# Two transformer blocks on one core: in the second routed layer, the weight pieces of two experts alternate in groups of eight

## The reference

```python
def moe_swiglu(x, w_router, w_gate, w_up, w_down):
    logits = (x @ w_router).astype(jnp.float32)
    top_val, top_idx = lax.top_k(logits, TOP_K)          # TOP_K = 2
    top_w = jax.nn.softmax(top_val, axis=-1)
    gate = jnp.einsum('bsk,bske->bse', top_w,
                      jax.nn.one_hot(top_idx, N_EXPERTS_2, dtype=jnp.float32)).astype(x.dtype)
    y = jnp.zeros_like(x)
    for e in range(N_EXPERTS_2):                         # 8 experts, inner width 3584
        h = jax.nn.silu(x @ w_gate[e]) * (x @ w_up[e])
        y = y + gate[..., e:e + 1] * (h @ w_down[e])
    return y
```

## Time and profile before

| | |
|---|---|
| three runs | 2212.12, 2214.03 (median), 2217.06 us |
| the profiled execution's own time | 2219.89 us |
| its span | 2218.1 us |
| TensorE busy | 2043.3 us (92%) |
| VectorE, ScalarE busy | 1248.8 us (56%), 991.1 us (45%) |
| HBM traffic over the span | 270 GB/s mean |
| this layer | from about 1236 us to about 2200 us |
| the three pairs | from about 1384 us to about 2094 us |

### The profile page before, as it was taken

How to read it: one execution, slowest core, us unless ns; L and a number is a source line. 1 busy time by engine, 2 the same in 40 slices (tenths; PEclk the granted TensorE clock), 3 DMA queues, 4 the chain that set the end, 5 groups by cost and what they waited for, 6 DMA issues and landing times. The chain is left out here.

```text
span 2218.1 us, 29794 instructions
## 1 busy us (share of the span) xinstructions
PE 2043.3 (92%) x11784; PEld 1520.7 (69%) x11784; DVE 1248.8 (56%) x1928; ACT 991.1 (45%) x1399; POOL 163.0 (7%) x151
## 2 busy tenths in 40 slices
PE   8998899999898889999989899999989998999896
PEld 8996885443687778997858687656645655665685
DVE  4557652221446676676276788544544544554787
ACT  3555442111244554442274567434443444443683
POOL 2103100000000003431001000000000000000000
PEclk9998998999998999999999999999999999999998
DMA  8650539999663244557502599999999999999994
GB/s 264 186 171 1 170 117 396 417 416 417 239 215 96 77 135 144 200 176 178 149 20 96 212 330 383 382 398 383 402 405 380 386 399 414 384 388 402 383 370 166
DMA packets 228364, 601.35 MB, mean 271 GB/s; under 512 B 16091, under 2 KB 121967, under 8 KB 205568
## 3 DMA queue, kind: packets, MB, share of 16 engines
q1 hardware_dynamic: 220112, 571.56, 69.0%
q0 software_dynamic: 8112, 27.91, 3.9%
HBM read 594.37 MB, written 5.05 MB: 270 GB/s over the span
## 5 line engine op out<-in xcount | busy, mean ns | idle before, releaser
L3426 DVE TENSOR_TENSOR ring_rounded<-ring,arena_rounded 128x1024 fp32r<-128x1024 f32 x268 | 312.5, 1219 | 37.5 <-ACT arena_rounded L2597 34.3
L2597 ACT ACTIVATE arena_rounded<-ring 128x1024 fp32r<-128x1024 f32 x268 | 270.9, 1059 | 50.1 <-DMA ring<-in_moe_w_down_dram 19.3
L2870 DVE TENSOR_TENSOR ring_rounded<-ring,ring_rounded 128x2048 fp32r<-128x2048 f32 (+1 forms) x68 | 147.1, 2165 | 160.4 <-ACT ring_rounded L2335 160.2
L1405 PE MATMUL psF<-ring_rounded,arena_rounded 128*128 128x512 f32 x512 | 202.6, 396 | 0.0
L2335 ACT ACTIVATE ring_rounded<-ring 128x2048 fp32r<-128x2048 f32 (+1 forms) x71 | 128.6, 1813 | 83.8 <-PE psF L1406 62.8
L1404 PE MATMUL psF<-arena_rounded 128*128 128x512 f32 x344 | 138.0, 401 | 8.2 <-ACT hT L2639 6.6
L3426 DVE TENSOR_TENSOR ring_rounded<-ring,memT_rounded 128x1024 fp32r<-128x1024 f32 x76 | 90.0, 1220 | 93.4 <-ACT memT_rounded L2597 93.1
L1406 PE MATMUL psF<-arena_rounded 128*128 128x512 f32 x344 | 136.8, 398 | 0.0
L2597 ACT ACTIVATE memT_rounded<-ring 128x1024 fp32r<-128x1024 f32 x76 | 78.2, 1060 | 92.3 <-DMA ring<-in_moe_w_down_dram 83.7
L1404 PE MATMUL psB<-yT_rounded,ring_rounded 128*128 128x256 f32 x384 | 112.5, 293 | 2.7 <-DVE ring_rounded L2870 2.7
L1405 PEld LDWEIGHTS psF<-ring_rounded,arena_rounded 128*128 128x128 f32 x512 | 96.9, 189 | 21.9
(11 more groups left out here) (584 smaller groups left out, 5060.1 us busy)
## 6 DMA issues: line engine op xcount, KB each, us to landing
ring<-in_moe_w_gate_dram SPq DMA_DIRECT2D x224, 512.0 KB, 8.1
ring<-in_moe_w_up_dram SPq DMA_DIRECT2D x224, 512.0 KB, 8.3
ring<-in_moe_w_down_dram SPq DMA_DIRECT2D x112, 1024.0 KB, 7.9
ring<-in_w_dram SPq DMA_DIRECT2D x48, 1024.0 KB, 16.4
arena<-in_w_dram SPq DMA_DIRECT2D x16, 1024.0 KB, 19.0
ring<-in_w_in_dram SPq DMA_DIRECT2D x14, 1024.0 KB, 5.4
ring<-in_ff_w_gate_dram SPq DMA_DIRECT2D x11, 1024.0 KB, 7.3
ring<-in_ff_w_up_dram SPq DMA_DIRECT2D x11, 1024.0 KB, 9.8
```

Of the source, the lines that this page charges most:

```text
L1405: mm(bank, x1, w2, start=False, stop=False, skip_group_check=open_groups)
L2597: ap_(piece(idx, w_hi).bitcast(R32), piece(idx, raw_halves), ACT.Copy).then_inc(piece_high, 1)
L2870: V.tensor_tensor(ring_r[:, slot_of[c], 0:kt * w].bitcast(R32), raw, ring_r[:, hi_slot[c], 0:kt * w], ALU.subtract).then_inc(weights_low, 1)
L3426: V.tensor_tensor(piece(idx, low_halves).bitcast(R32), piece(idx, raw_halves), piece(idx, w_hi), ALU.subtract).then_inc(piece_low, 1)
```

## The change

Only the order of work in the layer changes, on TensorE, ScalarE, VectorE and in the list of pieces that SyncE loads. The arithmetic is the same, and TensorE has the same number of matmuls.

- A pair step (the many step and the few step beside it) is now written out as one: gate many, turn of the few step before, down of it, up many, gate few, turn many, down many, up few. Groups of eight pieces of the two experts alternate.
- In the first step after a pair (`alone` with a few step before it), down of that few step comes before up instead of after it. Steps of an expert alone are otherwise in the old order.
- In a pair, `up` of a many step waits once, for the whole silu, and runs both halves of each piece together.
- After the last step, ScalarE and VectorE make the high and low parts of the last down pieces before they copy the turned block; they did so after it.

The core of the diff (the pieces' list, TensorE and ScalarE; VectorE's functions have the same form):

```diff
-        for t in range(n + 1):
-            for part, u in (("gate", t), ("up", t), ("down", t - 1)):
-                if not 0 <= u < n:
-                    continue
+        for t in range(n):
+            st, prev = self.steps[t], self.steps[t - 1] if t else None
+            if not st.alone:
+                parts = (("gate", t), ("down", t - 1), ("up", t), ("gate", t + 1), ("down", t), ("up", t + 1)) if st.big else ()
+            elif prev is None:
+                parts = (("gate", t), ("up", t))
+            elif prev.big:
+                parts = (("gate", t), ("up", t), ("down", t - 1))
+            else:
+                parts = (("gate", t), ("down", t - 1), ("up", t))
+            for part, u in parts + ((("down", t),) if t == n - 1 else ()):
...
+                    if not st.alone:
+                        pe.wait_ge(half_silu, order.halves[st.t] + 1)
+                        for j in range(st.pieces):
+                            hi, lo = big_piece(st.t, "up", j)
+                            for b in range(2):
+                                ins = many_product(X[0 if b else 2], j, hi, lo, 0, cols[b])
+                            ins.then_inc(piece_used, 1)
+                        return
...
+                def alone(st, prev):
+                    gate(st)
                     if prev is not None:
                         turn(prev)
...
+                        if not prev.big:
+                            down(prev)
+                    up(st)
...
+                    if st.first and st.pos == E2 - 1:
+                        mark_last()
+                    if prev is not None and prev.big:
                         down(prev)
+
+                def both(many, few, prev):
+                    gate(many)
+                    turn(prev)
+                    if many.first:
+                        turn_x(few.pos)
+                    down(prev)
+                    up(many)
+                    gate(few)
+                    turn(many)
+                    if many.last:
+                        turn_x(few.pos + 1)
+                    down(many)
+                    up(few)
...
+                def both(many, few, prev):
+                    silu(many)
+                    turned(prev)
+                    if many.first:
+                        save_x(few.pos)
+                    if many.first and many.pos > 1:
+                        save_y(steps[prev.t - 1])
+                    highs_of(prev.t, "down", range(8))
+                    highs_of(many.t, "up", range(8))
+                    if many.first:
+                        save_y(prev)
+                    silu(few)
+                    turned(many)
+                    if many.last:
+                        save_x(few.pos + 1)
+                    highs_of(many.t, "down", range(8))
+                    highs_of(few.t + 1, "gate", range(8))
...
+                highs_of(len(steps) - 1, "down", range(8))
+                turned(steps[-1])
```

More of the change, by code:

```diff
@@ L2154, in sorted_layer, with find_tokens @@
                 turn_x(0)
[L2156 to L2163, removed]
+                def find_tokens():
+                    pe.wait_ge(picks_ready, 1)
+                    for i in range(n_back):
+                        for t in range(TT):
+                            ins = mm(B[0][:, i:i + 1], all_picks[:, t, i, :], const("token")[:, t:t + 1],
+                                     start=(t == 0), stop=(t == TT - 1))
+                    ins.then_inc(tokens_found, 1)
@@ L2190, in sorted_layer @@
+                for t in range(begin):
+                    alone(steps[t], steps[t - 1] if t else None)
+                for t in range(begin, end, 2):
+                    both(steps[t], steps[t + 1], steps[t - 1])
+                alone(steps[end], steps[end - 1])
+                flag = [*crowded_flag(nc.tensor, layer)]
+                for t in range(end + 1, len(steps)):
+                    alone(steps[t], steps[t - 1])
+                turn(steps[-1])
+                down(steps[-1])
                 for k, (t, c) in enumerate(((0, 0), (0, 1), (1, 0), (1, 1))):
@@ L2648, in sorted_layer, with alone @@
                 first_sum(layer, ALPHA2, sum_started)
-                flag = []
-                for t in range(len(steps) + 1):
-                    st = steps[t] if t < len(steps) else None
-                    prev = steps[t - 1] if t else None
-                    if t == order.first_of[7] + 1:
-                        flag.extend(crowded_flag(nc.scalar, layer))
-                    if st is not None:
-                        silu(st)
+                def alone(st, prev):
+                    silu(st)
@@ L2657, in sorted_layer @@
                     if prev is not None:
                         turned(prev)
-                    if st is not None:
-                        if st.big and st.first and not st.alone or not st.big and st.last:
-                            save_x(st.pos + 1)
-                        highs_of(t, "up", range(4, 8))
-                    if t >= 2 and steps[t - 2].last and t != order.first_of[7] + 1:
-                        save_y(steps[t - 2])
-                    highs_of(t - 1, "down", range(8))
@@ new lines, in sorted_layer @@
+                begin, end = order.first_of[1], order.first_of[E2 - 1]
+                for t in range(begin):
+                    alone(steps[t], steps[t - 1] if t else None)
+                for t in range(begin, end, 2):
+                    both(steps[t], steps[t + 1], steps[t - 1])
+                alone(steps[end], steps[end - 1])
+                flag = [*crowded_flag(nc.scalar, layer)]
+                for t in range(end + 1, len(steps)):
+                    alone(steps[t], steps[t - 1])
```

111 lines of the change are left out of this document (62 added, 49 removed).

## The result

| | before | after |
|---|---|---|
| median | 2212.12 us (2207.14 to 2219.93, 19 runs) | 2217.68 us (2213.48 to 2224.22, 19 runs) |
| the profiled execution's own time | 2219.89 us | 2218.50 us |
| its span, mean granted clock | 2218.1 us, 0.958 | 2216.7 us, 0.961 |

The ratio of after to before is 1.0024 (interval 1.0013 to 1.0034): 5.6 us slower by the medians. The forecast was 2200 us, the range 2186 to 2214. The two traces alone say otherwise: the changed kernel's is 1.4 us *shorter*. It was taken 0.8 us above its kernel's median, the one of before 7.8 us above that of its 19 runs. Keep this difference in mind.

A forecast was written before the change was run, and what follows sets the result against it. The prediction held that TensorE and the weight stream, both nearly full, lose time in turn. Its terms gave -9.8 us with all falls, -27.5 with none; taking -14 us gave 2206, then 2200 us at the median, range 2186 to 2214.

The forecast's parts named there:

- The entry: First pair's first step: down of expert 0 moves ahead of up, costing +4.3 us, or +5.9 with a clock fall.
- The stops: Pair steps: TensorE waits 3.0 us ahead of down many and 1.3 us ahead of down few.
- all falls: Whole layer: the clock falls behind every longer new stop; the terms then sum to -9.8 us.
- The price of a fall: Behind each 3.0 us stop: the clock drops to 1.2 GHz and the matmuls lose 1.7 us.
- one pace: Rival, chance 0.18: the stream keeps its rate, rounds (one per pair of experts) stay 226.1 and 223.5 us; 2209 us.
- the prediction's signs: Trace checks: no pair stretch under 380 GB/s, 61 to 63 us between wide marks, expert 7's gate stop under 2 us.
- I take three falls in four: Total: between -9.8 us with every fall and -27.5 with none, it took -14 us.
- -8.1 us: Round three and entry to expert 7: the second gate's 6.61 us stop becomes 1.25 us; 217.7 us with falls.
- a stop like the 1.34 us one: Last down: its 2.98 us stop shrinks by 1.6 us and its fall, 1.6 us, goes; -3.2 us in all.
- -0.9, -3.5: Rounds one and two: 222.6 us each with all falls, against 223.5 and 226.1 in the profiled execution.
- 5.9 us off the total: Last step of the sum: the median stands 5.9 us below the profiled execution, so 2206 became 2200 us.
- the slower rival: Rival, chance 0.15: both stops of every pair step bring a fall, 2.4 and 1.6 us; +18 us, 2232 us.

The follow-up runs named there:

- e12: Kernel before with only the order within the pair steps alternated; entry into the pairs and end of the layer as before, nothing filled: 2219.68 us, 1.0025 of before.
- e2: Changed kernel, but in the first pair's first step down of expert 0 stays behind up many, as before: 2211.78 us, 0.9982 of before.
- e3: Changed kernel plus six matmuls of constants in the stop behind each turning of a many step in the pairs: 2202.52 us, 0.9935 of before.
- e6: Changed kernel with the third of the three products left out in the pairs, output less exact: 2194.42 us, 0.992 of before.
- e1: Changed kernel with the first two pieces' parts of down many made ahead of the few step's silu and turned block: 2210.87 us, 0.9984 of before.
- e11: e5 with nine instead of six matmuls of constants in each pair step: 2198.66 us, 0.9922 of before.
- e10: e5 with two low parts of expert 7's second gate made earlier, and only two of the last down's parts ahead of the turned copy: 2192.83 us, 0.9902 of before.
- e8: Kernel before, unchanged, run again for a second trace: 2219.58 us for the execution.
- e7: Kernel before with only the new end: down few ahead of up in expert 7's first step, last down's parts before the turned copy: 2208.44 us, 0.9981 of before.
- e5: Changed kernel with the old entry into the pairs and six matmuls of constants behind each many turning: 2194.65 us, 0.9914 of before.
- e9: Kernel before with eight matmuls of constants behind up of each wide few step, and the new end: 2204.34 us, 0.9947 of before.

## Why the prediction was wrong

**The sum, in ratios.** Alternation +0.25% (e12), new end beside it -0.43% (e2), new entry +0.42%: together +0.24%, the change, as it must be when each step is the difference of two kernels. The forecast was -14 us, -0.6%.

**The entry** was priced right by the trace (+4.3 or +5.9; measured +5.4). The ratios put it at 9 us, give or take 4.

**The stops** came as forecast: 2.99 for 3.0 ahead of down many, 1.25 for 1.3 ahead of down few in seven of twelve places (0.65 to 0.77 in the other five). So did the length of a round of the changed kernel: 222.6 forecast with all falls, 222.84 and 224.09 measured. The price of a fall, 1.7 us, was somewhat low (21.5 us behind eleven stops: 2.0 a fall). The rival *one pace*, by which the rounds keep 223.5 and 226.1 us, fell with the 216 to 220 us of e3 and e6; but the stream's floor is above the 214.8 to 217 us that the prediction had for it. Of the prediction's signs three came out against it: a stretch at 358 GB/s (none under 380 was to be seen), 63.5 and 63.6 us between two pairs of wide marks (61 to 63), and the stop of expert 7's gate (2.44 us, for under 2).

**The first failed step: "I take three falls in four".** Of the fifteen stops of 2.2 us and more from the entry on, thirteen had a fall behind them; the first ahead of down many and the last down's 2.21 us had none. (At the gate and at the last down it varies: a stop of 2.44 us at the gate had no fall in e1 and e11, and one of 2.19 at the last down had one in e1.) The two such stops in the trace of before both had one. To go below all falls had no row behind it, and made 4 of the 14 us.

**The second: round three, "-8.1 us".** The trace has -2.7 us up to the gate, and then a longer fall. VectorE ahead of expert 7's second gate, and TensorE at it (before: the earlier trace rows):

```profile
2091.24 1.28 DVE L3500 TENSOR_TENSOR arena<-arena,psF 128x512 f32<-128x512 f32 x2 [4.85 <-PE psF L1413]
2092.44 0.42 DVE L3577 CAST arena_rounded<-psB 128x256 fp32r<-128x256 f32 x1
2092.78 0.15 DVE L3578 COPY small<-psB 128x1 f32<-128x1 f32 x1
2092.84 3.49 DVE L3488 TENSOR_TENSOR ring_rounded<-ring,arena_rounded 128x1024 fp32r<-128x1024 f32 x3
```

```profile
2094.21 0.77 PE L1411 MATMUL psF<-arena_rounded 128*128 128x512 f32 x1 [2.44 <-DVE ring_rounded L3488]
```

The marks end at 2092.9, as forecast, but the gate also needs its first *low part*, which VectorE makes behind them: a stop of 2.44 us, not 1.25, and a fall of 6.1 us in place of 3.1, which no term had. Of the missing 5.4 us, 1.2 are the old fall behind the gate, which the prediction took off and a longer one replaced; 1.2 are the gate's stop; and the rest lies in the steps ahead: 0.9 in the two wide ones, 1.2 in the third, and 0.9 in the last stretch.

**The third: the last down, "a stop like the 1.34 us one".** It is 2.21 us. The turned low part (at 2192.61) stands behind the piece's low parts that were moved ahead of it:

```profile
2190.34 2.36 DVE L3488 TENSOR_TENSOR ring_rounded<-ring,mv_rounded 128x1024 fp32r<-128x1024 f32 x2
2192.61 0.68 DVE L3508 TENSOR_TENSOR PT_rounded<-psB,PT_rounded 128x512 fp32r<-128x512 f32 x1
```

From expert 7's second gate to the last scatter passed 106.6 us, against 107.5, and to the end of the span 122.5 against 123.9: -1.4 with the gate's longer fall, for -3.2. e10 put both queues right and found the forecast 1.26 and 1.41 us.

**The fourth, and the largest: the side of before.** The terms -0.9, -3.5 and -8.1 us set *modelled* rounds of the new order against *measured* rounds of one execution, which was 7.8 us above the median of 19 (5.9 above the three that were to be seen). Taking 5.9 us off the total only shifts both sides: if the rounds of that execution were slow, the savings were not there to be had. Three traces of the old order bear this out (before, e8, and e7 with the new end). Their eight stops of 3.83 to 3.85 us are the same, but the late matmuls of the three rounds lose 21.8, 19.4 and 15.6 us, and rounds one and two together take 449.7, 450.2 and 443.4 us. In the new order the loss is 21.5 and 20.3 us (after, e2), and the two rounds take 445.4 and 445.6 us (e12 and e2, with the old entry). So the old order varies by 7 us, and the trace that the prediction measured against is near its long end. Against the mean of the three, 447.8 us, the alternation is worth some 2 us in these rounds; -4.4 us stood in the forecast with a fall at every stop. How much of the 7.8 us lies in the rounds stays open, since what runs ahead of the pairs varies too: the step that both traces begin at 1395.4 begins at 1390.8 us in e7 and 1399.0 in e8, with the same work ahead of it.

**Where the expected gain went.** The stops of 3.84 us behind the runs of 24 went. In their place stand two stops a step, 2.99 and 1.25 us, and a fall. Filling shows what the falls cost: e3's rounds are 16.9 us shorter than after's, most of the 21.5 us that the late matmuls lose. The old order pays about as much, but filling brings it less (0.4%, where other stops with falls appear), and with both filled the alternation is ahead by 0.33% (e5 and e9, whose intervals just overlap). Thirteen of the fifteen stops of the longer kind brought a fall, and the slower rival with its price of 2.4 and 1.6 us a step, 2232 us, fell as well: the twelve stops of 0.65 to 1.28 us had none. The Trainium skill (TensorE: Matmul & The Clock Gate, HAM oscillation) tells of a kernel whose groups of matmuls each have a wait for a DMA of some 3 to 5 us behind them, and whose clock falls every time. This trace agrees for its stops of 2.4 us and more, with the one exception named; of stops as short as 1.25 us that section says nothing.

Slower had a chance of 0.13. From the forecast's -14 us to the measured +5.6 are 19.6 us: 4.2 for the falls left out, 5.4 for round three, 1.8 for the last down and what follows, 1.7 for rounds one and two, -0.5 for the entry, and 7.0 because the two profiled executions stood 7.8 and 0.8 us above their medians. Without the new entry the change would not have been slower (e2).

## What to carry to other kernels

Do not subtract a model of the new from one measured execution of the old: model both, or ask how far two executions of the old differ, and trust no term smaller than that. Where stops of 2 to 4 us remain after a reordering, count a fall of the clock behind each, and try a few matmuls of constants in the stop first: here twelve short blocks gave 0.9%, more than any reordering did, and in the unchanged order 0.4%. When a stop is shortened by moving work ahead on a queue, read what now stands behind it there: e1's silu, the gate's low part and the last turned copy were each a queue read too short.

## What the runs showed of the hardware that was not expected

- A fall's length does not follow the stop's: behind equal stops of 2.99 us in the changed kernel it was 3.1 to 5.7 us, and behind one of nine there was none; behind the stops of 3.84 us it was 2.7 to 6.1 us.
- Matmuls of constants with 256 columns, 0.22 us apart, keep the clock at 1.00 through a stop of 3.0 us; behind the 0.49 us that they leave open there is no fall (e3).
- The same work takes other times: ahead of the entry all kernels are alike, and the fourteen traces reach it between 1389.6 and 1399.1 us. Four runs of e10, with no fall from the entry to the last down, lie within 0.03% of each other, against 0.55% for 17 of before.
- The stream's own pace in the pairs is 410 GB/s, or 216 to 220 us a round, and leaving a third of the large products out does not change it.
